# Keeping the upper halves of the reused weights in HBM as well, and a later place for the keeping transfers

## The reference

```
h = RMSNorm(x);  z,q,k,v,glow,og = split(h @ w_in)          # w_in   1024 x 2064
a = causal pooling of z, then 4 maps 128 x 128
b = gated linear attention of q,k,v with decay from glow, normalised, times silu(og)
x = x + RMSNorm(concat(a, b) @ w_o)                          # w_o    1024 x 1024
u,g = split(RMSNorm(x) @ w_up)                               # w_up   1024 x 5632
x = x + RMSNorm((gelu(conv3(g)) * u) @ w_down)               # w_down 2816 x 1024
x = x + (p @ w_ple) * sigmoid(x @ w_ple_gate)                # w_ple_gate 1024 x 1024
```

## Time and profile before

| | value |
|---|---|
| median of three runs | 2620.07 us |
| profiled execution, its time | 2622.97 us |
| its span, first to last instruction | 2620.9 us |
| PE busy | 2573.7 us, 98% |
| DVE busy | 1587.7 us, 61% |
| ACT busy | 1353.8 us, 52% |
| DMA, 16 engines | 47.6% on SP's queue, mean 157 GB/s |
| mean granted TensorE clock | 0.993 |

### The profile page before, as it was taken

The page is one execution under the profiler, slowest core; times in us unless marked ns, Lnnn a source line. Parts: engine busy times, 40 slices in busy tenths (PEclk is TensorE's granted clock), DMA queues, the critical chain, the costliest instruction groups (busy, mean ns, idle before and its releaser), DMA issues.

```text
span 2620.9 us, 41342 instructions
## 1 busy us (share of the span) xinstructions
PE 2573.7 (98%) x16538; PEld 2508.3 (96%) x16538; DVE 1587.7 (61%) x2533; ACT 1353.8 (52%) x2156; POOL 164.1 (6%) x492
## 2 busy tenths in 40 slices
PE   7989999999999999999999999999999999999998
PEld 6889999999999999999999999999999999999997
DVE  5668855666665456666545666654566664547854
ACT  4545554555445456544445654444565444556554
POOL 3200000100000010000001000000100000000000
PEclk9999999999999999999999999999999999999999
DMA  5335546444434544443464444346444434755565
GB/s 167 114 105 171 167 140 200 160 162 141 152 125 123 204 142 162 151 148 122 125 207 140 166 146 153 121 121 207 145 161 145 145 125 124 260 180 194 187 180 196
DMA packets 121956, 411.76 MB, mean 157 GB/s; under 512 B 12735, under 2 KB 21095, under 8 KB 121767
## 3 DMA queue, kind: packets, MB, share of 16 engines
q1 hardware_dynamic: 121766, 409.13, 47.6%
HBM read 386.18 MB, written 22.89 MB: 156 GB/s over the span
## 4 chain that ended last, share of the span: by engine, by line
PE 94%; ACT 2%; DVE 2%; DMA 1%; issue 0%; SPq 0%; DVEq 0%; ACTq 0%
PE G L1645 29%; PE G L1647 28%; PE G L1646 28%; PE X L1704 2%; PE X L1641 2%; PE X L1638 2%; DMA w_lo<-kept_lo 1%; PE X L1831 1%; PE X L1759 1%; ACT w_hi L735 0%; PE X L1774 0%; DVE w_lo L1162 0%; DMA stage<-in_w_up_units_dram 0%; PE G L1638 0%; DVE A L1253 0%
## 5 line engine op out<-in xcount | busy, mean ns | idle before, releaser
L1645 PE MATMUL G<-h_hi,w_hi 128*128 128x384 f32 (+2 forms) x3264 | 1070.2, 328 | 17.2 <-DVE w_lo L1162 6.8
L1646 PE MATMUL G<-h_hi,w_lo 128*128 128x384 f32 (+2 forms) x3264 | 1052.1, 322 | 0.0
L1647 PE MATMUL G<-h_lo,w_hi 128*128 128x384 f32 (+2 forms) x3264 | 1052.0, 322 | 0.0
L735 ACT ACTIVATE w_hi<-stage 128x1024 fp32r<-128x1024 f32 (+1 forms) x500 | 519.0, 1038 | 398.4 <-DMA stage<-in_w_up_units_dram 237.4
L1162 DVE TENSOR_TENSOR w_lo<-stage,w_hi 128x1024 fp32r<-128x1024 f32 (+1 forms) x500 | 598.2, 1197 | 169.7 <-ACT w_hi L735 169.4
L1645 PEld LDWEIGHTS G<-h_hi,w_hi 128*128 128x128 f32 x3264 | 617.8, 189 | 23.7 <-issue 10.4
L1646 PEld LDWEIGHTS G<-h_hi,w_lo 128*128 128x128 f32 x3264 | 618.0, 189 | 1.7 <-issue 0.4
L1647 PEld LDWEIGHTS G<-h_lo,w_hi 128*128 128x128 f32 x3264 | 617.5, 189 | 0.0
L1645 PE MATMUL G<-y_hi,w_hi 128*128 128x384 f32 (+2 forms) x1056 | 346.3, 328 | 0.0
L1647 PE MATMUL G<-y_lo,w_hi 128*128 128x384 f32 (+2 forms) x1056 | 339.6, 322 | 0.0
L1646 PE MATMUL G<-y_hi,w_lo 128*128 128x384 f32 (+2 forms) x1056 | 339.5, 321 | 0.0
(11 more groups left out here) (234 smaller groups left out, 2676.5 us busy)
## 6 DMA issues: line engine op xcount, KB each, us to landing
stage<-in_w_up_units_dram SPq DMA_DIRECT2D x264, 512.0 KB, 3.5
w_lo<-kept_lo SPq DMA_DIRECT2D x112, 512.0 KB, 4.5
stage<-in_w_down_units_dram SPq DMA_DIRECT2D x96, 448.0 KB, 3.4
w_whole<-in_w_in_units_dram SPq DMA_DIRECT2D x72, 512.0 KB, 3.6
stage<-in_w_o_units_dram SPq DMA_DIRECT2D x48, 512.0 KB, 3.4
stage<-in_w_down_units_dram SPq DMA_DIRECT2D x48, 512.0 KB, 3.5
w_whole<-in_w_gate_units_dram SPq DMA_DIRECT2D x40, 512.0 KB, 3.6
stage<-in_w_in_units_dram SPq DMA_DIRECT2D x24, 512.0 KB, 4.3
```

The lines of the kernel that those rows point to most:

```text
L735: act.activation(w_hi[s][:, 0:parts, :], whole[:, 0:parts, :], ACT.Copy).then_inc(hi_made, 1)
L1645: pe.matmul(ps[:, 0:w], l_hi, r_hi[:, 0:w], start=start, stop=False)
L1646: pe.matmul(ps[:, 0:w], l_lo, r_hi[:, 0:w], start=False, stop=False)
L1647: return pe.matmul(ps[:, 0:w], l_hi, r_lo[:, 0:w], start=False, stop=stop)
```

## The change

Three things change. First, a second HBM buffer, kept_hi, takes the hi halves of the same 24 units: those of `in` are written in tile 1, those of `gate` in tile 0. From `in` of tile 2 and `gate` of tile 1 on (LOADS_HI, 104 units), SP loads hi from kept_hi instead of the whole weight, ScalarE makes nothing, and TensorE waits for the landing itself. Second, `keeper` is gone: lo of all 16 `in` units is kept in tile 0, and all of tile 1's `in` units load it. Third, the keeping moves: `keep_halves(n - SLOTS)` now issues the keeping of unit n - 4 in `load_unit(n)`, directly ahead of the load that waits for it.

```diff
-def keeper(unit):
-    return unit[2] % 2 if unit[1] == "in" else 0
-KEEP_LO = [unit[1:] in KEPT_NO and unit[0] == keeper(unit) for unit in UNITS]
-LOADS_LO = [unit[1:] in KEPT_NO and unit[0] > keeper(unit) for unit in UNITS]
+KEEP_LO = [unit[0] == 0 and unit[1:] in KEPT_NO for unit in UNITS]
+KEEP_HI = [unit[1:] in KEPT_NO and unit[0] == (1 if unit[1] == "in" else 0) for unit in UNITS]
+LOADS_LO = [unit[0] > 0 and unit[1:] in KEPT_NO for unit in UNITS]
+LOADS_HI = [lo and not hi for lo, hi in zip(LOADS_LO, KEEP_HI)]
+HIS_MADE = list(itertools.accumulate(not loaded for loaded in LOADS_HI))
...
-            def keep_los(n):
-                for k in range(keep_next[0], n + 1):
-                    if KEEP_LO[k]:
-                        sp.wait_ge(lo_made, LOS_MADE[k])
-                        sp.dma_start(kept_lo[...], exact(w_lo[k % SLOTS][:, :, :])).then_inc(kept[k % SLOTS], 16)
-                keep_next[0] = n + 1
+            def keep_halves(n):
+                s, name = n % SLOTS, UNITS[n][1:]
+                if KEEP_HI[n]:
+                    sp.wait_ge(hi_made, HIS_MADE[n])
+                    sp.dma_start(kept_hi[KEPT_NO[name]], exact(w_hi[s][:, :, :])).then_inc(kept[s], 16)
+                if KEEP_LO[n]:
+                    sp.wait_ge(lo_made, LOS_MADE[n])
+                    sp.dma_start(kept_lo[KEPT_NO[name]], exact(w_lo[s][:, :, :])).then_inc(kept[s], 16)
             def load_unit(n):
                 if n >= SLOTS:
-                    keep_los(n - SLOTS + 1)
+                    keep_halves(n - SLOTS)
                     sp.wait_ge(*end_tick(UNITS[n - SLOTS]))
-                    if KEEP_LO[n - SLOTS]:
+                    if KEEP_LO[n - SLOTS] or KEEP_HI[n - SLOTS]:
                         sp.wait_ge(*keeping(n - SLOTS))
                 if LOADS_LO[n]:
-                    sp.dma_start(w_whole[s][:, :, :], source(unit)).then_inc(landed[s], 16)
+                    if LOADS_HI[n]:
+                        sp.dma_start(exact(w_hi[s][:, :, :]), kept_hi[j]).then_inc(landed[s], 16)
+                    else:
+                        sp.dma_start(w_whole[s][:, :, :], source(unit)).then_inc(landed[s], 16)
                     sp.dma_start(exact(w_lo[s][:, :, :]), kept_lo[j]).then_inc(landed[s], 16)
...
             def one_hi(n):
-                if n < len(UNITS):
+                if n < len(UNITS) and not LOADS_HI[n]:
...
             def halves_ready(n):
-                if LOADS_LO[n]:
-                    pe.wait_ge(hi_made, n + 1)
+                if LOADS_HI[n]:
+                    pe.wait_ge(*landing(n))
+                elif LOADS_LO[n]:
+                    pe.wait_ge(hi_made, HIS_MADE[n])
```

More of the change, by code:

```diff
@@ L154, in hybrid_layer @@
                  w_in_units, w_o_units, w_up_units, w_down_units, w_ple_units, w_gate_units,
-                 kept_lo, y_prompt, y_sample, pool_prompt, gla_prompt, conv_prompt, pool_sample, gla_sample,
+                 kept_hi, kept_lo, y_prompt, y_sample, pool_prompt, gla_prompt, conv_prompt, pool_sample, gla_sample,
                  conv_sample):
@@ L442, in keeping @@
         def keeping(n):
-            return kept[n % SLOTS], 16 * sum(KEEP_LO[k] for k in range(n % SLOTS, n + 1, SLOTS))
+            return kept[n % SLOTS], 16 * sum(KEEP_LO[k] + KEEP_HI[k] for k in range(n % SLOTS, n + 1, SLOTS))
         def tick(name):
@@ L459, in _ @@
         def _(sp):
-            keep_next = [0]
             def source(unit):
@@ L468, in source @@
                         "gate": w_gate_units}[kind][m]
-            def keep_los(n):
-                for k in range(keep_next[0], n + 1):
-                    if KEEP_LO[k]:
-                        sp.wait_ge(lo_made, LOS_MADE[k])
-                        sp.dma_start(kept_lo[KEPT_NO[UNITS[k][1:]]], exact(w_lo[k % SLOTS][:, :, :])).then_inc(
-                            kept[k % SLOTS], 16)
-                keep_next[0] = n + 1
+            def keep_halves(n):
[6 more added lines that the diff above has]
+                    sp.dma_start(kept_lo[KEPT_NO[name]], exact(w_lo[s][:, :, :])).then_inc(kept[s], 16)
             def load_unit(n):
@@ L481, in load_unit @@
                 if n >= SLOTS:
-                    keep_los(n - SLOTS + 1)
+                    keep_halves(n - SLOTS)
                     sp.wait_ge(*end_tick(UNITS[n - SLOTS]))
-                    if KEEP_LO[n - SLOTS]:
+                    if KEEP_LO[n - SLOTS] or KEEP_HI[n - SLOTS]:
                         sp.wait_ge(*keeping(n - SLOTS))
                 if LOADS_LO[n]:
-                    s = n % SLOTS
-                    sp.dma_start(w_whole[s][:, :, :], source(unit)).then_inc(landed[s], 16)
-                    sp.dma_start(exact(w_lo[s][:, :, :]), kept_lo[KEPT_NO[unit[1:]]]).then_inc(landed[s], 16)
+                    s, j = n % SLOTS, KEPT_NO[unit[1:]]
+                    if LOADS_HI[n]:
+                        sp.dma_start(exact(w_hi[s][:, :, :]), kept_hi[j]).then_inc(landed[s], 16)
+                    else:
+                        sp.dma_start(w_whole[s][:, :, :], source(unit)).then_inc(landed[s], 16)
+                    sp.dma_start(exact(w_lo[s][:, :, :]), kept_lo[j]).then_inc(landed[s], 16)
                     return
@@ L1160, in one_lo @@
                     s, parts = n % SLOTS, parts_of(UNITS[n])
-                    dve.wait_ge(hi_made, n + 1)
+                    dve.wait_ge(hi_made, HIS_MADE[n])
                     dve.tensor_tensor(w_lo[s][:, 0:parts, :], stage[s][:, 0:parts, :], exact(w_hi[s][:, 0:parts, :]),
@@ L2141 @@
         args.append(nc.dram_tensor(f"in_{name}_dram", a.shape, F32, kind="ExternalInput").ap())
-    args.append(nc.dram_tensor("kept_lo", (len(KEPT_NO), P, KD, P), F32, kind="Internal").ap())
+    for name in ("kept_hi", "kept_lo"):
+        args.append(nc.dram_tensor(name, (len(KEPT_NO), P, KD, P), F32, kind="Internal").ap())
     for n, shape in enumerate(_OUTS):
```

## The result

The changed kernel takes 2646.05 us (median of 4 runs, 2643.8 to 2649.27); the kernel before took 2620.14 us over the same number. The ratio is 1.0097 with a 95% interval of 1.008 to 1.0115, so the change costs 26 us. The profiled execution took 2644.54 us with a span of 2642.8; that of before was among the slower of its runs and this one among the faster, so the two spans differ by 21.9 us and not by 26.

The account below looks back on a forecast made before the run. TensorE, busy 98% of the span, was taken to bound the kernel. Losses of 3 (tile 0), 15.5 (tile 1) and 6.5 (late gates) less 8 of relief sum to +17 us: 2637 from the median 2620.07; range 2617 to 2657.

Parts of the forecast that it names:

- The loop on SP: Where units are kept, each load waits for the keep just issued: turns of 5.8 us, 7.1 with three transfers.
- Tile 1: `in` units and what follows: turns of 7.1 us make unit 115 12.5 us late; 15.5 us lost (0 to 28).
- a slack: SP's loads: issued when unit n - 4 ends, wanted when unit n starts, three units later.
- Late gates: Units 124 to 129: five turns of 7.1 us make unit 129 4.9 us late; 6.5 us lost (1 to 13).
- Tile 0: `in` units, turns of 5.8 us: unit 18's hi copy delays emptying the sample outputs; 3 us lost (0 to 6).
- The relief: Tiles 2 to 5 and the end: ScalarE's hi copies go, shortening TensorE's waits, mostly for `ple` results; 8 us gained.
- the ceiling: Most that removing ScalarE's copies could return, from `ple` waits, slow clock and y_tok: 10.5 us.
- A: No change: writes hide behind reads, turns of 6.4 us for three transfers; 2617.5 us, chance 0.12.
- B: Faster: turns under TensorE's 5.75 us, ScalarE's relief at its ceiling, no stall left; -9, 2611 us, chance 0.08.
- C: Much slower: a third transfer costs what the second did, turns of 8.0 us; +35, 2655 us, chance 0.14.

Follow-up runs that it names:

- the early keeps: Changed kernel with its keeping transfers back at their old place (unit n - 3, not n - 4, kept in the load of unit n): 2606.62 us, 0.9946.
- the pair on one chip: Changed kernel with keeps at their old place, rerun with all 24 hi halves kept (2607.6 us) and with only the gates' hi kept and loaded (2609.47 us).

## Why the prediction was right, and where it was off

**The loop on SP.** Right: it bound exactly where keeps stand, from unit 96 on and no longer at unit 116, and the early keeps show that taking it away takes the whole loss away. The turn was forecast at 7.1 us; it is 7.1 to 7.4 in most turns, and one of 9.0 and one of 7.8 bring the mean to 7.47. Tile 0's turn was forecast at 5.8 and is 5.8 over units 5 to 18. At the late gates SP issued the loads of units 124 and 129 34.9 us apart, against five turns of 7.1, 35.5.

**Tile 1.** This is the term that was mis-sized: 15.5 forecast, 24.1 measured. Two causes, both in the runs. First, the turn was 0.4 us too short over 13 turns, 5 us. Second, I priced the end of the loop by when a unit is usable for TensorE, with "a slack: it is issued when unit n - 4 ends and wanted when unit n starts, three units later"; that gave 12.5 us at unit 115. That slack isn't there. The first engine that wants unit 110 is ScalarE, two units ahead and in an order that it can't leave, and its slack was 2.6 us. By the forecast's own turns unit 110 lands at 523.6, and ScalarE began its copy at 505.89: 17.7 us and not 12.5. Measured are 22.5, plus 1.6 for the slow clock behind the wait, for which 1.7 had been put. I had seen this order inside the `in` units (unit 103 delayed by 10 us; it was 15.4) and not carried it on to `ple` 0 and the gates.

**Late gates.** 8.3 us against 6.5, by the mechanism given: unit 129 is late for its own weights, 3.8 us, the longest wait for w_lo in that window, with the clock at 0.50 until 5.8 us behind it.

**Tile 0.** +2.9 against +3, and this closeness is in part luck. The sample outputs came 2.7 us later, as priced (119.30 against 116.61 us), but by then TensorE had already stood idle in the `in` units, where I had put nothing: for 1.0 us at 79 us and 2.5 us at 96 us, waits that the kernel before doesn't have. And one profile of each kernel says little here: the eight kernels with the changed kernel's keeps in tile 0 took 309.3 to 312.9 us, the four with the same keeps at the early place 302.7 to 305.3, and before's single profile 306.4.

**The relief.** 12.5 us against 8, above the ceiling of 10.5. It is where it was said to be: 0.8 at each `ple` 0 of tiles 1 to 3, 3.7 and 0.9 at tile 4's two `ple` units, 3.5 at tile 5's, 1.6 at the last gates, and 0.4, unpriced, in tile 5's `in`. The big terms were right (3.7 for 3.8, 3.5 for 3.4). The ceiling was too low because each of the four short `ple` waits, 0.5 to 0.6 us long, gave back 0.8 to 0.9; why they give back more than their length isn't shown. That hi never read back costs 15 us shows the relief as a whole, and the pair on one chip that it is the gates'.

**The rivals.** A needed turns of 6.4 us and B turns under TensorE's 5.75; they were 7.47. B's price was also off by its own words: the relief at its ceiling is 10.5 us, not 9. C was right about tile 1's size (26) but not by its mechanism, since the third transfer cost 1.5 us and not 2.3.

The forecast came from the profiled execution of before, whose 2622.97 us were 2.9 above the median. The misses, 8.6 and 1.8 us too little loss, 4.5 too little relief, leave 5.8 us on the sum of the stages and 9 on the medians. That the total came this close is in part luck: the under-priced relief cancelled 4.5 of the 10.4 us by which the losses were under-priced.

**A version that beats both.** The early keeps with the kept hi: 2606.62 and again 2607.6 us, ratios 0.9946 and 0.9952 (0.9938 to 0.9966). Keeping hi of the gates alone comes to the same within 2 us in the pair on one chip (2609.47 against 2607.6), with 16 keeps fewer.

## What to carry to other kernels

A queue that waits for a transfer it has just issued becomes a loop, and its turn is that transfer's time to land, with what was issued just ahead of it; compare the turn with the pace of the engine it feeds, and put one independent item between issue and wait. To see how much lateness a ring of buffers absorbs, look for the first engine that waits for the landing in its own order, here a helper that works two units ahead, and take its slack (2.6 us) and not that of the last consumer. Work taken off an engine that is half idle paid only where that work stood directly ahead of something awaited: here 40 of 104 copies did nearly all of it.

## What the runs showed of the hardware that I had not expected

A keep written to HBM behind two loads lands 6.3 us after its issue, behind one load 5.4; with transfers crowding it, as in the early keeps, 6.8, while the core moved 266 GB/s over 92 us and TensorE lost nothing. The third transfer of a turn thus cost about 1.5 us (turns of 5.8 with two, of 7.3 with three), close to the 1.3 us that 512 KB need at the measured peak of 414 GB/s.
